# Prompt attention: scores three tiles ahead, and most of the combination of the two maps on GpSimd

## The reference, cut to what matters

```python
s = jnp.einsum('bqhmd,bkhmd->bhmqk', qs, ks).astype(F32) * (DIFF_DH ** -0.5)
s = s + bias[None, :, None]
s = jnp.where(rel >= 0, s, jnp.finfo(F32).min)
p = jax.nn.softmax(s, axis=-1)
a = p[:, :, 0] - lam * p[:, :, 1]
return jnp.einsum('bhqk,bkhd->bqhd', a, v.astype(F32))
```

## Time and profile before

| what | value |
|---|---|
| median of 3 runs | 3785.05 us (3784.03 to 3786.7) |
| the profiled execution: time, span | 3788.77 us, 3787.0 us |
| mean granted TensorE clock, whole program | 0.959 of full |
| busy over the span: PE, DVE, ACT, POOL | 3424.4, 1771.8, 1099.7, 118.9 us |
| attention stretch | 2173 to 3014 us of the span, 841 us |
| busy in it: PE, DVE, ACT, POOL | 715.75, 700.06, 539.24, 0 us |

### The profile page before, as it was taken

The page is one execution under the profiler, slowest core; times in us unless marked ns, Lnnn a source line. Parts: engine busy times, 40 slices in busy tenths (PEclk is TensorE's granted clock), DMA queues, the critical chain, the costliest instruction groups (busy, mean ns, idle before and its releaser), DMA issues. The chain is left out here.

```text
span 3787.0 us, 54465 instructions
## 1 busy us (share of the span) xinstructions
PE 3424.4 (90%) x19319; PEld 2764.8 (73%) x19319; DVE 1771.8 (47%) x4120; ACT 1099.7 (29%) x1875; POOL 118.9 (3%) x158
## 2 busy tenths in 40 slices
PE   9999997995999989999999888888888778589999
PEld 7888995773888868888888666666666645378887
DVE  2123113555555542111113388887888734455554
ACT  2111102332121212111111166666666522311111
POOL 0000002110000000000000000000000000000000
PEclk9999998997999999999999989999999988799999
DMA  4621213336222224122221311111110088622221
GB/s 169 87 79 64 81 48 103 116 103 227 87 78 84 77 78 137 70 73 73 77 78 60 93 43 46 41 46 41 45 40 12 15 316 311 232 85 76 89 76 48
DMA packets 199098, 350.72 MB, mean 93 GB/s; under 512 B 19005, under 2 KB 109918, under 8 KB 198894
## 3 DMA queue, kind: packets, MB, share of 16 engines
q1 hardware_dynamic: 198894, 348.04, 27.9%
HBM read 243.50 MB, written 104.47 MB: 92 GB/s over the span
## 5 line engine op out<-in xcount | busy, mean ns | idle before, releaser
L362 PE MATMUL in_ps_y<-in_w_hi,in_x_hi 128*128 128x512 f32 (+2 forms) x1920 | 725.3, 378 | 0.0
L366 PE MATMUL in_ps_y<-in_w_hi,in_x_lo 128*128 128x512 f32 (+2 forms) x1920 | 722.2, 376 | 0.0
L364 PE MATMUL in_ps_y<-in_w_lo,in_x_hi 128*128 128x512 f32 (+2 forms) x1920 | 722.1, 376 | 0.0
L366 PEld LDWEIGHTS in_ps_y<-in_w_hi,in_x_lo 128*128 128x128 f32 x1920 | 361.5, 188 | 60.4
L362 PEld LDWEIGHTS in_ps_y<-in_w_hi,in_x_hi 128*128 128x128 f32 x1920 | 361.8, 188 | 59.8 <-ACT in_out L437 0.6
L364 PEld LDWEIGHTS in_ps_y<-in_w_lo,in_x_hi 128*128 128x128 f32 x1920 | 361.7, 188 | 58.9
L506 DVE COPY in_out<-in_ps_y 128x512 f32<-128x512 f32 (+2 forms) x88 | 56.7, 645 | 686.2 <-PE in_ps_y L366 647.0
L1819 DVE TENSOR_SCALAR_CACHE_REDUCE att_s<-att_ps_s,att_far 128x256 f32<-128x256 f32 (+3 forms) x608 | 328.4, 582 | 43.5 <-PE att_ps_s L1665 35.4
L1692 PE MATMUL att_ps_o<-att_v,att_a_t 128*128 128x128 f32 x2176 | 305.6, 289 | 32.5 <-ACT att_a_t L1753 31.6
L1692 PEld LDWEIGHTS att_ps_o<-att_v,att_a_t 128*128 128x128 f32 x2176 | 268.7, 196 | 85.5 <-ACT att_a_t L1753 58.5
L1741 ACT ACTIVATE att_s<-att_s,att_neg 128x128 f32<-128x128 f32 (+15 forms) x256 | 306.8, 1199 | 7.7 <-DVE att_neg L1836 7.6
(11 more groups left out here) (256 smaller groups left out, 4792.4 us busy)
## 6 DMA issues: line engine op xcount, KB each, us to landing
smp_k_pg<-in_cache_k SPq DMA_DIRECT2D x64, 512.0 KB, 5.7
smp_v_pg<-in_cache_v SPq DMA_DIRECT2D x64, 512.0 KB
res_factors<-factors SPq DMA_DIRECT2D x34, 512.0 KB
res_o<-mixer_out SPq DMA_DIRECT2D x34, 512.0 KB, 4.5
factors<-in_out SPq DMA_DIRECT2D x64, 256.0 KB, 2.0
in_stage<-in_diff_w_in SPq DMA_DIRECT2D x16, 1024.0 KB, 8.5
gla_x<-gla_qka SPq DMA_DIRECT2D x17, 520.0 KB, 3.5
gla_v<-gla_v SPq DMA_DIRECT2D x17, 512.0 KB, 4.3
```

The source lines that it names most:

```text
L362: nc.tensor.matmul(bank[:, cols], x_hi[:, k, rows], w_hi[:, k, cols], start=(k == 0), stop=False)
L364: nc.tensor.matmul(bank[:, cols], x_hi[:, k, rows], w_lo[:, k, cols], start=False, stop=False)
L366: mm = nc.tensor.matmul(bank[:, cols], x_lo[:, k, rows], w_hi[:, k, cols], start=False, stop=(k == KD - 1))
```

## The change

`AHEAD = 3`: TensorE now issues `scores` of tile i+3 in iteration i, and again `turn` and `meet` of tile i. VectorE issues `take` of tile i+2 and `combine` of tile i+1 in iteration i; ScalarE's code for the order of `exps`, `copies` and `output` is untouched. `HELD = 4`: there are four buffers of `s_sb`, so `take` waits for the tile four back. The combination is split by columns: VectorE combines the first 128 keys, and GpSimd all others of the tile, in two instructions, a multiplication by the weight in place and an addition. `turn` of group 0 waits for both. The weight has two buffers. Tile 0 has one block of keys, so GpSimd has no part in it.

```diff
+    AHEAD, HELD = 3, 4
-        s_sb = [sb(f"s{i}", [P, 2, SEQ]) for i in range(2)]
+        s_sb = [sb(f"s{i}", [P, 2, SEQ]) for i in range(HELD)]
+        def wait_turned(eng, H, i):
+            if i >= 2:
+                eng.wait_ge(s["a_turned"], after(GROUPS * H + first_group[i - 1]))
+            elif not (isinstance(H, int) and H == 0):
+                eng.wait_ge(s["a_turned"], after(GROUPS * H - sum(groups[T - 1 + i:])))
+        def own(i):
+            return 1
...
                 def turn(H, i, g):
                     if g == 0:
-                        pe.wait_ge(s["a_done"], after(T * H + i + 1))
+                        pe.wait_ge(s["a_done"], after(HELD + T * H + i + 1))
+                    if g == own(i) // 4 and own(i) <= i:
+                        pe.wait_ge(s["a_pooled"], after(HELD + pooled(H, i)))
...
-                        if not (last and i + 2 >= T):
-                            ahead_to = ahead(H, u, i, 2)
+                        if not (last and i + AHEAD >= T):
+                            ahead_to = ahead(H, u, i, AHEAD)
...
+            @block.gpsimd
+            def _(pool):
+                def combine(H, u, i):
+                    cols = slice(own(i) * P, (i + 1) * P)
+                    if own(i) > i:
+                        return
+                    pool.wait_ge(s["weight_done"], after(T * H + i + 1))
+                    stand_alone(pool, core)
+                    nc.gpsimd.tensor_scalar(s_sb[i % HELD][:, 1, cols], s_sb[i % HELD][:, 1, cols],
+                                            weight[i % 2][:, :], None, ALU.mult).then_inc(s["a_weighed"], 1)
+                    wait_turned(pool, H, i)
+                    pool.wait_ge(s["a_weighed"], after(pooled(H, i)))
+                    nc.gpsimd.tensor_tensor(a[i % 2][:, cols], s_sb[i % HELD][:, 0, cols],
+                                            s_sb[i % HELD][:, 1, cols], ALU.add).then_inc(s["a_pooled"], 1)
...
                 def combine(H, u, i):
-                    n = (i + 1) * P
+                    n = own(i) * P
                     dve.wait_ge(s["exp_done"], after(2 * (T * H + i + 1)))
...
                 def head(H, u, last):
                     for i in range(T):
+                        if not (last and i + 2 >= T):
+                            take(*ahead(H, u, i, 2))
                         if not (last and i + 1 >= T):
-                            take(*ahead(H, u, i, 1))
-                        combine(H, u, i)
+                            combine(*ahead(H, u, i, 1))
```

More of the change, by code:

```diff
@@ L59, in __init__ @@
         self.passed = {e.engine: nc.alloc_semaphore(name=f"passed_{i}")
[L60 removed]
+                       for i, e in enumerate((nc.vector, nc.tensor, nc.sync, nc.gpsimd))}
     def sem(self, name):
@@ L1544, in attention @@
         inv = [sb(f"inv{i}", [P, 2]) for i in range(2)]
-        weight = sb("weight", [P, 1])
+        weight = [sb(f"weight{i}", [P, 1]) for i in range(2)]
         o_sb = [sb(f"o{i}", [P, D_VD]) for i in range(2)]
@@ L1724, in _ @@
                     prep(0, n, is_q, g, turn_banks)
-                for i in range(2):
+                for i in range(AHEAD):
                     for _ in scores(0, 0, i):
@@ L1783, in _, with head @@
                 over_heads(act, head)
+            @block.gpsimd
[12 more added lines that the diff above has]
+                                            s_sb[i % HELD][:, 1, cols], ALU.add).then_inc(s["a_pooled"], 1)
+                def head(H, u, last):
+                    for i in range(T):
+                        if not (last and i + 1 >= T):
+                            combine(*ahead(H, u, i, 1))
+                pool.sem_inc(s["a_pooled"], HELD)
+                combine(0, 0, 0)
+                over_heads(pool, head)
             @block.vector
@@ L1803, in take @@
                         dve.wait_ge(head_in[u], after(48 * (H // 2 + 1) if isinstance(H, int) else 24 * (H - u) + 48))
-                    if not (isinstance(H, int) and H == 0 and i == 0):
-                        dve.wait_ge(s["a_done"], after(T * H + i - 1))
+                    dve.wait_ge(s["a_done"], after(T * H + i + 1))
+                    dve.wait_ge(s["a_pooled"], after(HELD + pooled(H, i - HELD)))
                     n_keys = (i + 1) * P
@@ L1826, in take @@
                                 ins = nc.vector.tensor_tensor_reduce(
-                                    out=s_sb[i % 2][:, m, start:hi_], in0=ps_s[n % RING][:, start - lo_:hi_ - lo_],
+                                    out=s_sb[i % HELD][:, m, start:hi_], in0=ps_s[n % RING][:, start - lo_:hi_ - lo_],
                                     in1=bias[u][:, NEAR - (n_keys - start):NEAR], scale=1.0, scalar=-3.0e38,
@@ L1867, in _ @@
                 take(0, 0, 0)
+                take(0, 0, 1)
+                combine(0, 0, 0)
                 over_heads(dve, head)
```

22 lines of the change are left out of this document (13 added, 9 removed).

## The result

The changed kernel takes 4379.82 us (median of 4 runs, 4377.43 to 4384.05); the kernel before, in 4 runs of its own, 3785.88 us. The ratio is 1.1568, with a 95% interval of 1.1548 to 1.1588: 594 us slower. I had forecast 4196 us and a range that ended at 4330 us. The sign was right and the size too small by 184 us.

What follows compares the result with a forecast made beforehand. Bound by a round between TensorE and VectorE, neither full. 148.5 us a head against 105.1, times 8, gave +347 us; 3788.8 + 347 + 64 for the clock made 4200 us profiled, 4196 us median; range 4090 to 4330.

Steps and rivals of the forecast that it cites:

- The chain: Attention rounds: turn, copies, second exponential, combine, take and TensorE's next scores stand in one line; forecast sum +347 us.
- Steps 1 to 4: Iteration i: TensorE turns tile i, then needs a bank; VectorE's take(i+3) follows combine(i+1), whose exponential waits behind tile i's copies.
- The third step: TensorE's third step of scoring tile i+3 blocks until VectorE frees a bank; at i=12, 6.2 us after the turn starts.
- The clock: Attention stage: mean clock 0.87, 40 us of each head at half clock cost 8 us, +64 us in all.
- The end that I gave for the clock: Upper end of the attention stage's clock cost: +120 us, at a clock of 0.78.
- GpSimd's multiplication: In GpSimd's combination, priced like the affine select, 0.84 ns a column; exposed only at tiles 14 and 15, 28 us.
- My dear end: GpSimd's multiplication as dear as its addition: 4.7 us a head on tiles 14 and 15, 37 us in all.
- Rival 1: Attention stage: same lost overlap as forecast, but the clock holds at 0.95: 4136 us; chance 0.20.
- Rival 2: VectorE's 128-key combining instruction waits for GpSimd's whole multiplication, delaying take(i+3): +99 us, 4295 us; chance 0.23.
- Rivals 3 and 4: Third step of scores does not block, exponentials done in time: 3702 us, chance 0.04; or no change, chance 0.01.

Runs made afterwards that it cites:

- e3_exps_ahead: The changed kernel with ScalarE making the exponentials of tile i+2 in iteration i instead of tile i+1: 3792.12 us, ratio 1.0018.
- e4_fill: The changed kernel with 20 unused identity transposes on TensorE before the third step of scores, when tile i+3 has three or four steps: 4302.64 us.
- e5_no_mult: The changed kernel without GpSimd's multiplication by the weight, second map added unweighted beyond the first 128 columns: 4288.42 us, ratio 1.1324.
- e6_fill_more: The changed kernel with 32 unused transposes at the blocked third step and 36 ahead of the scores of iterations 14 and 15: 4250.04 us, ratio 1.1229.
- e12_chain: The changed kernel without GpSimd's multiplication, with 32 unused transposes at the third step and 16 in iterations 14 and 15: 4168.11 us, ratio 1.101.
- e7_port_free: e3_exps_ahead with VectorE's negation split into two one-column instructions and the weight made from one array and two pointers: 3784.91 us, ratio 0.9995.

## Why the prediction was right in its mechanism and wrong in its size

**The chain: right.** Steps 1 to 4 of the forecast are the timeline above, line by line, and e3_exps_ahead, which moves only the exponentials, takes 588 of 594 us away. The third step stood 5.18, 6.02 and 5.67 us behind the transposes of tiles 9, 10 and 11, where I had 5.05, 5.4 and 5.8. Tile 10 is late because the preparation of the next head (0.60 us, from 2823.43 to 2824.03) lies between the combination and the take in even rounds; I had not put it there. Over tiles 5 to 12 of that head the third step stood 44.9 us behind the transposes in all, against 43.0 in the forecast. With fill, at a clock of 0.98 and 0.97, these rounds take 90.3 and 90.5 us, and the forecast's sum was 88.2 us.

**The clock: the step that failed.** "At a mean clock of 0.87, 40 us of a head at half clock cost 8 us: +64 us." Both numbers in it were too small. The mean was 0.74, which is 93 us of a head at half clock and not 40. The fill brings the stage from 0.74 to 0.89, by which about 460 of its microseconds are no longer at half clock, and gives back 130 us: an estimate of 0.28 us for each (0.34 by e4_fill, at 0.81), where I had 0.2. The first error is the larger one, a factor of 2.3 beside 1.4. In the trace the work behind the waits takes the loss: in the fourth head the rounds of tiles 5 to 12 have 61.1 us behind the third steps, at 0.69, where the forecast had 45.2. The end that I gave for the clock, +120 us, was below the 130 us that the fill alone gives back.

The row from which I had worked out 0.38 us for each microsecond at half clock was misread. The two heads of the earlier trace rows differ by 5.05 us, but 3.26 us of that lie in the round of tile 15, where both had full clock:

```profile
2384.57:2395.10 10.53, 7.29 (x60) 6.33 (x58) 1.92 (x11) 4.10 (x11) 0.00 (x0) 0.99 0.22 64
2709.03:2716.30 7.27, 6.96 (x60) 6.30 (x58) 1.90 (x10) 3.97 (x11) 0.00 (x0) 1.00 0.03 10
...
2393.74 0.63 PE L1643 MATMUL att_ps_k<-ident,att_k_nat 128*128 128x128 f32 x4 [2.93 <-issue]
```

The first has TensorE standing still for 2.93 us before the next head's preparation, and the second does not. That leaves 1.8 us for 13 us at half clock, 0.14 each. There the half clock lay in the small tiles, and the row did not carry over to work behind a wait in every round.

**GpSimd's multiplication: the second term mis-sized.** "I take the select's price for the multiplication (one array in, one out)" was 0.84 ns a column; it is 2.52. My dear end, the price of the addition, was also too cheap, since the multiplication costs more than it: 5.231 against 4.222 us at 1920 columns. It was worth 28 us in my sum and 91 us in e5_no_mult, where the forecast's own chain would have given some 80 us at the measured 4.91 and 5.23 us of tiles 14 and 15 ((4.91 + 5.23) x 8). The addition, at 4.222 us, was sized rightly (0.2 + 1920 x 2.1 ns = 4.23 us). That the price falls on tiles 14 and 15 alone was right.

**The sum for one head.** The forecast's head without clock, and the fifth head of the changed kernel and of two others, in us:

| rounds of tiles | forecast | after | e6_fill_more | e12_chain, no multiplication |
|---|---|---|---|---|
| 0 to 4 | 32.2 | 36.3 | 36.2 | 36.5 |
| 5 to 12 | 88.2 | 105.7 | 90.3 | 90.5 |
| 13 to 15 | 28.1 | 38.8 | 36.0 | 27.8 |
| sum, us | 148.5 | 180.7 | 162.5 | 154.8 |

32.2 us are missing in this head; the forecast had 8 of them for the clock. Of the 32.2, the fill returns 15.4 + 2.8 = 18.2, taking the multiplication away returns a further 8.2 in tiles 13 to 15 (I had counted 3.5 for it), and 2 to 4 us in each of the three parts were neither. In tiles 0 to 4 the clock was at 0.59 in all three kernels and no fill was tried; how much of their 4 us is clock and how much chain stays open. So does the rest of the clock's price: the fills reach 0.89 and 0.90 in the stage, not the 0.95 of before.

e12_chain's 4168 us beside the forecast's 4196 - 28 = 4168 us without the multiplication is partly luck: my +64 us for the clock stands there for those small terms and for what is left of the clock.

**The rivals.** Rival 1 (the clock holds) fell with the 0.74. Rival 2, VectorE's 128-key instruction held by GpSimd's multiplication, did not occur in the changed kernel: it takes 0.352 us in all 128 cases, since VectorE starts 0.08 us before GpSimd (2823.16 and 2823.24). The mechanism is real, though. In the changed kernel it hit the negation (0.583 us), off the path; in e3_exps_ahead the weight too, and from e7_port_free on the combining instruction itself. Rivals 3 and 4 fell with the wait of 316.8 us. Rival 3's condition, exponentials that are done in time, is what e3_exps_ahead creates, and even then the time was not under that of before until the holds and the reciprocal's buffers were dealt with.

**The range** was too narrow above: it let the clock's and the multiplication's dear ends stand for one another (4330 us), where both came true together and beyond their ends.

## What to carry to other kernels

When one engine is moved further ahead, list for each of its partners what its in-order queue holds in front of the instruction that the mover now needs; here ScalarE's exponential stood behind copies of the tile that TensorE had just postponed, and moving it by one tile was worth 588 of 594 us. A new wait on TensorE that returns in every round is priced with the work behind it at a lower clock (0.69 here), not with the wait alone. Before a cost is read from two stretches, check that they differ in nothing else: 3.26 of my 5.05 us stood where both had full clock. Before work is given to GpSimd, measure the very operation at two sizes and see that its pair lies a round off the path: the same split cost 36 us inside the loop and gained 39 us outside it.

## What the runs showed of the hardware

**VectorE's tiny instructions wait for GpSimd's long ones.** A fp32 `tensor_scalar` on two columns in SBUF, 0.17 us alone, lasted 3.51 us and ended 0.02 us after GpSimd's multiplication; an instruction with two SBUF arrays of one column likewise (0.22 to 3.15 us). The reciprocal on two columns ran in 0.17 us while GpSimd's addition was under way, and the `tensor_scalar` on one column in 0.154 us on average; none of the 256 in e7_port_free took more than 0.156 us, though 156 began while a GpSimd instruction ran. The Trainium skill (SBUF — State Buffer, "Who interferes with whom") gives the rule of an exclusive lock held for the whole instruction; these rows agree. The Trainium skill (VectorE: DVE Perf Modes, "What auto-detection actually checks") makes the mode in which a one-array instruction uses both ports depend on the outermost dimension of more than one element, even or equal in source and destination. Two columns meet that and one column has no such dimension, and these rows agree with it. That VectorE's side is the victim even for two numbers per partition is the part to remember: 128 such instructions grew by 82 us in all in e3_exps_ahead (0.806 against 0.169 us) and by 53 us in the changed kernel (0.583).

**A one-array multiplication on GpSimd is dearer than a two-array addition**: 5.231 against 4.222 us at 1920 fp32 columns, with a factor per partition. The Trainium skill (GPSIMD Engine Reference, "4.1 Engine selection") calls one-input work there roughly line-rate. This case's rows disagree, and the measurement decides.

**The clock is lower in the work behind a wait than in the wait.** In the round of tile 10 it was 0.97 up to the end of the wait and 0.59 behind it; over all 64 such waits 0.86 and 0.69. Matmuls of the same shape took 0.79 us at 1.2 GHz and 0.40 us at 2.4 GHz. Transposes of no use, put into the wait, brought the rounds of tiles 5 to 12 from 0.76 to 0.98 and made them 15.4 us shorter in the fifth head.
